# Square sums on GpSimd, a row norm for the memory, a reordered opening, two moved steps, and the turned probabilities of the differential heads on ScalarE

## The chip, the cores and the metric

One core of a Trainium2 chip runs the whole program once. The metric is the device time of one execution in microseconds (us), the median of three runs. The engines are PE (TensorE, matrix products), DVE (VectorE), ACT (ScalarE), POOL (GpSimd) and SP (SyncE, which here only issues DMAs). They run beside each other, each in the order of its own program, and meet at semaphores.

## What is computed

A transformer stack of width 1024 over 256 tokens, in float32, of which only the parts that the change touches are shown.

```python
def rmsnorm(x, g):
    xf = x.astype(jnp.float32)
    y = xf * lax.rsqrt(jnp.mean(xf * xf, axis=-1, keepdims=True) + EPS)
    return (y * g.astype(jnp.float32)).astype(x.dtype)

# first block
h = rmsnorm(x, norm_mix_g[l])
x = x + gated_branch_mixer(h, w_in[l], ...)              # begins with h @ w_in: a_val, a_gate, ...
x = x + memory_cross_attention(rmsnorm(x, norm_x_g[l]), rmsnorm(mem, norm_mem_g[l]), ...)
x = x + hierarchical_moe(rmsnorm(x, norm_ffn_g[l]), ...)  # 16 experts in 4 groups
# second block, layer 0 (sparse attention heads) and layer 1 (differential heads)
h = rms_norm(x, ln_mix_g[i]) * (1.0 + sc1[:, None, :]) + sh1[:, None, :]
x = x + g1[:, None, :] * y                                # y: the attention of the layer
h = rms_norm(x, ln_mlp_g[i]) * (1.0 + sc2[:, None, :]) + sh2[:, None, :]
x = x + g2[:, None, :] * (jnp.square(jax.nn.relu(h @ w_mlp_in[i])) @ w_mlp_out[i])
# differential heads: 8 heads of two softmaxes
p = masked_softmax(s, kpos[None, :] <= t[:, None])
a = p[:, :, 0] - lam * p[:, :, 1]
o = jnp.einsum('bhqk,bhkd->bhqd', a.astype(v.dtype), v)
o = rms_norm(o, subln_g) * (1.0 - lam_init)
```

`sc` and `sh` come from a product of a 1024-vector with a 1024x6144 matrix per layer (`w_ada`), the "modulation".

## The kernel before

**Products in three parts.** Activations lie turned: 128 features on the partitions, 256 tokens along the row, eight such blocks (KB = 8). A float32 product is made of three products of the fp32r type: high weights by high activations, high by low, low by high. ACT makes the high part of a weight panel (`w_hi`, `ahead`, line 1505) and of an activation, DVE the low part as the rest (`w_lo`, `ahead`, line 2045; `e_lo`, `h_lo`). A weight panel of 128x2048 elements (1 MB) is brought by a DMA on SP's queue (`load_panel`, line 515) into one of a ring of raw buffers, in the order of a plan. A panel's load waits until PE has finished with the panel that held the buffer. PE, ACT and DVE each go through the panels in the same order, and where in its program an engine makes its part of a panel is written out by hand.

**Norms.** For a norm over the 1024 features, ACT squares the blocks in pairs (128x512 each), and PE adds over the partitions by products with a matrix of ones, which leaves the sum on all partitions: `stat_pair(tag, j)` (line 847) waits for the j-th pair of squares and makes two products of 256 columns, so that a norm has 8. They stand between the panels that PE works on while the squares come in. ACT then takes the square root (`root`, line 1586) and DVE the reciprocal. Five norms, called x, ffn, m0, d and m1, are made "raw" (`raw_first`, line 729): PE doesn't wait for the square root but multiplies the residual, with its gains, and the factor is put on the result afterwards. For them ACT makes the high part of each block (`raw_act`, line 1546) and DVE the low one (`raw_low`, line 2109). PE takes each block with six products. The last pair of squares is waited for between the fourth block and the fifth; for d, later pairs stand behind the second, fourth and fifth block. `split_norm` (line 2084) is a norm that is not raw, `scaled` (line 2075) one whose result is not split.

**The opening.** SP's queue (`loads`, line 498) issues the identity, the two halves of x, panel 0, nine rows of small vectors, panel 1; then it waits until all 18 small vectors have landed (the other nine are on ACT's queue), issues the memory (1 MB), and goes on with panel 2. ACT gets the sums of squares of the rows of x by an accumulating square (128x1024, one per half). DVE puts their reciprocal roots on a diagonal, PE spreads them with the ones matrix and turns the small vectors, DVE takes them out of PSUM, splits panel 0 and makes the eight scaled blocks (`split_norm`, the call at line 2173). PE makes a_gate (two panels), then turns the memory in sixteen 128x128 transposes, and makes a_val. The memory's blocks are squared (`squares_of`), summed by 8 ones products behind a_val (`stats`, line 858), and scaled by `scaled("mem", ...)`; they are used after the gates, near 150 us.

**GpSimd** has little to do: it makes the windowed sums of the pooling branch (line 585), issues the 64 DMAs of the modulation matrix (`ada_loads`, line 608; each waits for DVE to have used the piece before), issues small constants, computes one gain vector (line 633), and makes the low part of two panels of d_o.

**The experts** (16, three panels each) run two deep. DVE and ACT make each expert's hidden activation, DVE multiplies it with the row of its gate, and PE needs its high (`e_hi`) and low part (`e_lo`). Pieces of the modulation (`ada(l, n)`, line 2450: 1 or 2 DVE operations of 128x1536 each) are put between DVE's other steps by hand, in the expert stage for layer 0, in the first MLP for layer 1.

**The differential heads.** Per head h: scores on PE, maxima on DVE (`d_max`), exponentials on ACT (`d_exp`, two), the normalized difference on DVE (`d_norm`, line 2840), three transposes on PE (`d_turned`) into PSUM, one copy of 128x384 out of it (on ACT for even h, on DVE for odd h), and the products with the values on PE (`d_values`, line 1419). Every second head ACT squares and copies the output of a pair of heads (`d_out`, line 1995). Behind the last head come a root, a reciprocal and spreads on PE, and the panels of d_o, with `keep_busy` products as filler where PE would stand still.

## Time and profile before

| what | value |
|---|---|
| time, median of 3 runs (lowest, highest) | 1316.54 us (1315.47, 1316.83) |
| the profiled execution: time | 1315.27 us |
| its span in the trace | 1313.5 us |
| PE busy | 1290.3 us, 98% |
| DVE busy | 950.7 us, 72% |
| ACT busy | 657.9 us, 50% |
| GpSimd busy | 88.5 us, 7% |
| chain that ended last, by engine | PE 86%, DVE 8%, ACT 3%, issue 2% |

The span is what the trace covers; the time of the same execution is 1.8 us longer. The granted TensorE clock was 0.998 of full speed. How a row of a timeline is read: start in us from the span's beginning, duration in us, engine, line of the kernel, operation, tile out<-tiles in, size out<-size in, and x with the number of instructions that the row covers; a bracket gives the engine's wait right before and what it waited for. In a group's row the numbers behind the bar are busy us, mean ns of one instruction, and idle us before them. `arena` is one large SBUF buffer that many stages share, so its name stands for different things in different rows; `ring` and `acc` are PSUM banks, and L675, L1503 are helpers that record most products and activations.

### The profile page before, as it was taken

To read this page: it belongs to the slowest core of one execution; us is meant where nothing else is said; L and a number is where in the kernel's file an instruction comes from. 1 tells how busy PE (TensorE), PEld (TensorE's weight loads), DVE (VectorE), ACT (ScalarE), POOL (GpSimd) and SP (SyncE) were. 2 spreads that over 40 slices of the span, in tenths; PEclk is the share of its full clock that TensorE was granted. 3 is DMA by queue.
4 is the path that set the end of the run, shared out by engine and by line. 5 is a ranking of instruction groups with operands and counts; after the bars stand their busy time and mean duration, and the time that the engine had idled before them with its cause. 6 is when DMAs were issued, how large, how long until landed. Compare 5 with 4: busy or idle time off the path is not lost.

```text
span 1313.5 us, 24511 instructions
## 1 busy us (share of the span) xinstructions
PE 1290.3 (98%) x10581; PEld 1237.9 (94%) x10581; DVE 950.7 (72%) x1199; ACT 657.9 (50%) x872; POOL 88.5 (7%) x134
## 2 busy tenths in 40 slices
PE   7999999999999999999999999999999999999998
PEld 7999999999999999999989689999999888999998
DVE  5769897764797667777776978877789666754443
ACT  4544436364643434343657747454456455654441
POOL 4003000000000000020100000100000020000000
PEclk9999999999999999999999999999999999999999
DMA  9665555545488777885632046999875431465550
GB/s 280 202 206 176 182 176 166 187 135 179 161 288 297 258 258 267 284 284 166 209 128 92 6 161 225 322 313 325 312 235 168 165 97 65 161 192 193 180 174 33
DMA packets 172701, 259.67 MB, mean 198 GB/s; under 512 B 5157, under 2 KB 147794, under 8 KB 172594
## 3 DMA queue, kind: packets, MB, share of 16 engines
q1 hardware_dynamic: 160906, 203.13, 47.1%
q0 software_dynamic: 10848, 53.69, 11.6%
q8 instruction: 84, 1.38, 0.4%
q10 hardware_dynamic: 840, 1.28, 0.3%
q14 instruction: 23, 0.19, 0.1%
HBM read 257.03 MB, written 1.05 MB: 196 GB/s over the span
## 4 chain that ended last, share of the span: by engine, by line
PE 86%; DVE 8%; ACT 3%; issue 2%; DMA 1%; SPq 0%; POOL 0%; ACTq 0%; DVEq 0%
PE ring L675 59%; PE acc L675 24%; ACT w_hi L1503 2%; DVE w_lo L2051 2%; PE acc L1276 1%; DVE arena L2100 1%; PE ring L1085 1%; DMA raw<-in_w_in_dram 1%; ACT h_hi L1503 1%; ACT arena L1503 1%; DMA arena<-in_w_ada_dram 1%; DVE arena L2464 0%; DVE h_lo L2096 0%; DVE h_lo L2094 0%; DVE norm L2066 0%
## 5 line engine op out<-in xcount | busy, mean ns | idle before, releaser
L675 PE MATMUL ring<-h_hi,w_hi 128*128 128x256 f32 (+1 forms) x2016 | 575.0, 285 | 5.7 <-DVE w_lo L2051 1.8
L675 PE MATMUL ring<-h_hi,w_lo 128*128 128x256 f32 (+1 forms) x2016 | 568.2, 282 | 0.0
L675 PE MATMUL ring<-h_lo,w_hi 128*128 128x256 f32 (+1 forms) x2016 | 566.5, 281 | 0.0
L2051 DVE TENSOR_TENSOR w_lo<-raw,w_hi 128x2048 fp32r<-128x2048 f32 x189 | 430.9, 2286 | 165.4 <-ACT w_hi L1503 164.7
L1503 ACT ACTIVATE w_hi<-raw 128x2048 fp32r<-128x2048 f32 x191 | 363.2, 1905 | 132.1 <-PE ring L675 64.0
L675 PEld LDWEIGHTS ring<-h_hi,w_hi 128*128 128x128 f32 x2016 | 379.8, 188 | 11.8 <-issue 7.3
L675 PEld LDWEIGHTS ring<-h_lo,w_hi 128*128 128x128 f32 x2016 | 380.7, 189 | 2.6 <-issue 2.2
L675 PEld LDWEIGHTS ring<-h_hi,w_lo 128*128 128x128 f32 x2016 | 380.9, 189 | 0.0
L675 PE MATMUL acc<-e_hi,w_hi 128*128 128x256 f32 x768 | 216.9, 282 | 2.9 <-DVE e_lo L2752 1.5
L675 PE MATMUL acc<-e_hi,w_lo 128*128 128x256 f32 x768 | 215.1, 280 | 0.0
L675 PE MATMUL acc<-e_lo,w_hi 128*128 128x256 f32 x768 | 215.1, 280 | 0.0
L1503 ACT ACTIVATE arena<-ring 128x512 f32<-128x512 f32 (+3 forms) x106 | 61.1, 582 | 245.0 <-PE ring L675 232.6
L675 PEld LDWEIGHTS acc<-e_hi,w_hi 128*128 128x128 f32 x768 | 144.4, 188 | 4.5 <-DVE e_lo L2499 1.8
L675 PEld LDWEIGHTS acc<-e_lo,w_hi 128*128 128x128 f32 x768 | 144.6, 188 | 0.0
L675 PEld LDWEIGHTS acc<-e_hi,w_lo 128*128 128x128 f32 x768 | 144.5, 188 | 0.0
L2464 DVE SCALAR_TENSOR_TENSOR arena<-arena,cond 128x1536 f32<-128x1536 f32 x56 | 101.6, 1813 | 5.8 <-DMA arena<-in_w_ada_dram 4.3
L606 POOL DMA_DIRECT2D arena<-in_w_ada_dram x64 | 33.8, 529 | 561.9 <-DVE arena L2464 327.4
L2752 DVE TENSOR_TENSOR e_lo<-arena,e_hi 128x512 fp32r<-128x512 f32 x32 | 22.1, 691 | 62.3 <-ACT e_hi L1503 62.3
L1503 ACT ACTIVATE e_hi<-arena 128x512 fp32r<-128x512 f32 x48 | 29.8, 621 | 63.4 <-DVE arena L2494 63.1
L2230 DVE SCALAR_TENSOR_TENSOR arena<-arena,vec 128x256 f32<-128x256 f32 x120 | 54.7, 524 | 0.0
L675 PE MATMUL ring<-arena 64*128 64x128 f32 (+5 forms) x370 | 52.0, 352 | 0.9 <-ACT arena L1503 0.8
L1503 ACT ACTIVATE arena<-ring,stat 128x128 f32<-128x128 f32 (+1 forms) x104 | 42.8, 428 | 16.8 <-DVE stat L2659 9.3
(317 smaller groups left out, 1348.2 us busy)
## 6 DMA issues: line engine op xcount, KB each, us to landing
arena<-in_w_ada_dram POOLq DMA_DIRECT2D x64, 768.0 KB, 6.3
raw<-in_w_mlp_in_dram SPq DMA_DIRECT2D x32, 1024.0 KB, 5.8
raw<-in_w_mlp_out_dram SPq DMA_DIRECT2D x32, 1024.0 KB, 5.0
raw<-in_w_in_dram SPq DMA_DIRECT2D x24, 1024.0 KB, 5.8
raw<-in_w_e_gate_dram SPq DMA_DIRECT2D x16, 1024.0 KB, 6.3
raw<-in_w_e_up_dram SPq DMA_DIRECT2D x16, 1024.0 KB, 5.4
raw<-in_w_e_down_dram SPq DMA_DIRECT2D x16, 1024.0 KB, 5.0
raw<-in_diff_w_in_dram SPq DMA_DIRECT2D x12, 1024.0 KB, 5.3
```

The costliest lines, as they stand in the source:

```text
L606: pool.dma_start(flat(ADA_RAW, (n % 2) * ADA_W, ADA_W), src).then_inc(S(f"ada_landed{n % 2}"), 16)
L675: return nc.tensor.matmul(dst, lhs, rhs, start=start, stop=stop, **kw)
L1085: last = nc.tensor.transpose(bank(f)[:, j * P:(j + 1) * P], src, ident[:])
L1276: last = nc.tensor.transpose(dst[:, c * P:(c + 1) * P], src[:, c * P:(c + 1) * P], ident[:])
L1503: return nc.scalar.activation(dst, src, fn, **kw)
L2051: tt(w_lo[q % RAW][:, 0:n], raw[q % RAW][:, 0:n], w_hi[q % SPL][:, 0:n].bitcast(F32), ALU.subtract)\
L2100: stt(blk(mid, 8)[:, b], x_t[:, b, :], gain(b), norm[:, row, :], ALU.mult, ALU.mult)\
L2230: chain.did(stt(y[:, b], at, w, y[:, b], ALU.mult, ALU.add))
L2464: last = stt(done_at if k == KB - 1 else so_far, piece, cond[:, k:k + 1], so_far, ALU.mult, ALU.add)
L2752: tt(e_lo[:, s, :].rearrange("p b t -> p (b t)"), hid(2 + c % 2), e_hi[:, s, :].rearrange("p b t -> p (b t)").bitcast(F32), ALU.subtract). ...
```

## The change

**Square sums.** For the norms x, ffn, m0, d and m1, GpSimd adds the squares of the first six blocks: `fold_two` adds pair 1 to pair 0 (128x512), `fold_rest` adds pair 2 (128x512) and then the two halves of the result (128x256). PE then makes one product with the ones matrix for that sum and two for the last pair: `stat_sums`, at the place in `raw_first` where the last pair was before (for d: behind the seventh block). All `stat_pair` calls go, and the function too.

**Where GpSimd does it.** x: ahead of the wait for `xo_ready`. ffn: inside `ada_loads(0)`, behind the second piece's DMA. m0: inside `ada_loads(1)`, `fold_two` behind the fourth piece, `fold_rest` behind the pieces ahead of the loop. d: behind `ada_loads(1)`. m1: behind the two splits of d_o.

**The mix norm's gain** gets a transpose of its own (`mix_gain`, 8 columns), so that the norm doesn't wait for all small vectors. DVE makes the norm's first two blocks, then the low part of panel 0, then the rest; the take-out of the other vectors comes behind panel 1. Panel 1 is split in two halves (ACT and DVE), and PE starts on the first as soon as it is there (`two_halves`).

**The memory** is normed by rows: ACT makes accumulating squares of the landed rows (two of 128x1024) and a root, DVE a reciprocal and two row scalings of 128x1024, PE turns the scaled rows, and DVE multiplies each block with its gain as it takes it out of PSUM (8 of 128x256 in place of 4 of 128x512). The 8 ones products, `squares_of("mem")`, `root("mem")` and `scaled("mem")` go. SP's queue issues panel 2 ahead of the memory's DMA.

**Two orders.** In the expert stage the split of the panel behind the first expert's moves ahead of the wait for the gate row, on DVE and on ACT, and one modulation piece moves behind the product with the gate row. In the MLP `chunk_lo(1)` moves ahead of the modulation piece `ada(1, 4)`.

**The differential heads.** ACT makes the PSUM copy of every head, DVE none. Some semaphores become several in turn (`sig`), with no other effect.

```diff
 def loads
             load_panel(sp, turn, 1)
-            sp.wait_ge(S("vecs_landed"), 16 * N_VEC_DMA)
+            sp.wait_ge(S("vecs_landed"), 16 * (N_VEC_DMA - 1))
+            load_panel(sp, turn, 2)
 on GpSimd
+            def fold_two(tag):
+                pool.wait_ge(*sig(tag + "_squared", 2))
+                nc.gpsimd.tensor_tensor(sq[:, 0:2], sq[:, 0:2], sq[:, 2:4], ALU.add).then_inc(S(tag + "_folded"), 1)
+            def fold_rest(tag):
+                pool.wait_ge(*sig(tag + "_squared", 3))
+                pool.wait_ge(*sig(tag + "_folded", 1))
+                nc.gpsimd.tensor_tensor(sq[:, 0:2], sq[:, 0:2], sq[:, 4:6], ALU.add).then_inc(S(tag + "_folded"), 1)
+                pool.wait_ge(*sig(tag + "_folded", 2))
+                nc.gpsimd.tensor_tensor(sq[:, 0], sq[:, 0], sq[:, 1], ALU.add).then_inc(S(tag + "_folded"), 1)
 ada_loads
                     ada_load(turn, l, n, at(n))
+                    if n == (1, 3)[l]:
+                        fold_two(("ffn", "m0")[l])
+                        if l == 0:
+                            fold_rest("ffn")
+                if l == 1:
+                    fold_rest("m0")
 raw_first on PE
-                    for j in sums.get(k, ()):
-                        stat_pair(tag, j)
+                    if k == sums:
+                        stat_sums(tag)
+            def stat_sums(tag):
+                f, sq = FL[tag + "_stat"], blk(SQX, 8)
+                open_fill(f)
+                pe.wait_ge(*sig(tag + "_folded", 3))
+                mm(bank(f)[:, 0:T], ones[:], sq[:, 0], True, False)
+                pe.wait_ge(*sig(tag + "_squared", 4))
+                mm(bank(f)[:, 0:T], ones[:], sq[:, 6], False, False)
+                mm(bank(f)[:, 0:T], ones[:], sq[:, 7], False, True).then_inc(S(tag + "_summed"), 1)
 PE, the opening
-            keep_busy(FL["a_gate"], 8)
-            full("a_gate", split="mix_ready", together=1)
-            pe.wait_ge(S("mem_landed"), 16)
+            keep_busy(FL["a_gate"], 4)
+            linear_first([PN["a_gate"]], FL["a_gate"], block_ready("mix_ready"))
+            two_halves(PN["a_gate"] + 1, FL["a_gate"] + 1)
+            pe.wait_ge(S("mem_rows"), 2)
             turn_rows(lambda i: acc[i], 2048, "mem_turned")
             full("a_val")
-            stats("mem", lambda k: blk(SQ + k)[:, 0], "mem_squared")
 PE, three of the places of the sums
-            raw_first("ffn", PN["moe"], half_bank(moe_fill(0)), {3: (3,)})
+            raw_first("ffn", PN["moe"], half_bank(moe_fill(0)), 3)
-                raw_first(f"m{l}", PN[name], lambda b: acc[b], {3: (3,)})
+                raw_first(f"m{l}", PN[name], lambda b: acc[b], 3)
-            raw_first("d", PN["d_q"], lambda b: acc[b], {1: (0, 1), 3: (2,), 4: (3,)})
+            raw_first("d", PN["d_q"], lambda b: acc[b], 6)
 ACT, the opening
-            ahead(2 - SPL)
+            act.wait_ge(S("raw_landed1"), 16)
+            for b, sem in ((0, "first_half_hi"), (1, "hi_made")):
+                c = slice(b * P, (b + 1) * P)
+                func(w_hi[1][:].rearrange("p (k n) -> p k n", k=KB)[:, :, c], raw[1][:].rearrange("p (k n) -> p k n", k=KB)[:, :, c],
+                     ACT.Copy).then_inc(S(sem), 1)
+            act.wait_ge(S("mix_ready"), KB)
+            act.wait_ge(S("mem_landed"), 16)
+            for t in range(2):
+                last = func(blk(SQ + 4 * t, 4), arena[:, 2048 + t * D:2048 + (t + 1) * D].rearrange("p (b t) -> p b t", b=4),
+                            ACT.Square, accum_out=stat[:, 4 + t:5 + t])
+            func(stat[:, 6:8], stat[:, 4:6], ACT.Sqrt, scale=1.0 / D, bias=eps[:]).then_inc(S("mem_squared"), 1)
             ahead(0)
 DVE, the opening
+            split_norm("mix", lambda b: mix_gain[:, b:b + 1], mid=SQ, row=2, behind_two=lambda: ahead(1 - SPL))
+            dve.wait_ge(S("mem_squared"), 2)
+            chain.did(nc.vector.reciprocal(stat[:, 6:8], stat[:, 6:8]))
+            chain.settle()
+            for t in range(2):
+                rows = arena[:, 2048 + t * D:2048 + (t + 1) * D]
+                ts(rows, rows, stat[:, 6 + t:7 + t], None, ALU.mult).then_inc(S("mem_rows"), 1)
 DVE, the experts
+            ahead(PN["moe"] + 1)
             dve.wait_ge(S("cond_made"), 1)
-            for n in range(2):
-                ada(0, n)
+            ada(0, 0)
             row_wait(0)
             tt(act0, act0, row, ALU.mult).then_inc(S("act_made"), 1)
-            ahead(PN["moe"] + 1)
+            ada(0, 1)
             expert_lo(0)
 DVE, the MLP
                 ahead(PN[name] + 1)
+                chunk_lo(1)
                 if l == 0:
                     ada(1, 4)
-                chunk_lo(1)
                 ahead(PN[name] + 2)
 ACT, the differential heads
             for h in range(DIFF_HEADS):
-                if h % 2 == 0:
-                    act.wait_ge(S("d_turned"), h + 1)
-                    func(d_pt(h), acc[2][:, 0:3 * P], ACT.Copy).then_inc(S("d_pt_even"), 1)
-                elif h > 2:
+                act.wait_ge(S("d_turned"), h + 1)
+                func(d_pt(h), acc[2 + h % 2][:, 0:3 * P], ACT.Copy).then_inc(S(("d_pt_even", "d_pt_odd")[h % 2]), 1)
+                if h % 2 and h > 2:
                     d_out(h // 2 - 1)
 DVE, the differential heads
-                if h % 2:
-                    dve.wait_ge(S("d_turned"), h + 1)
-                    nc.vector.tensor_copy(d_pt(h), acc[3][:, 0:3 * P]).then_inc(S("d_pt_odd"), 1)
```

## Rows read from the trace of the kernel before

**Rows 1.** The page: busy time by engine, and one of its costliest groups.
```profile
PE 1290.3 (98%) x10581; PEld 1237.9 (94%) x10581; DVE 950.7 (72%) x1199; ACT 657.9 (50%) x872; POOL 88.5 (7%) x134
...
L2051 DVE TENSOR_TENSOR w_lo<-raw,w_hi 128x2048 fp32r<-128x2048 f32 x189 | 430.9, 2286 | 165.4 <-ACT w_hi L1503 164.7
```

**Rows 2.** PE's timeline: start us, duration us, instruction; in brackets the wait before.
```profile
26.29 0.39 PE L675 MATMUL ring<-h_hi,w_hi 128*128 128x256 f32 x1 [1.84 <-DVE w_lo L2051]
...
338.54 0.35 PE L675 MATMUL ring<-h_hi,w_hi 128*128 128x256 f32 x1 [1.03 <-DVE h_lo L2094]
...
362.94 0.39 PE L675 MATMUL acc<-e_hi,w_hi 128*128 128x256 f32 x1 [1.18 <-DVE e_lo L2499]
...
819.26 0.39 PE L675 MATMUL acc<-e_hi,w_hi 128*128 128x256 f32 x1 [1.52 <-DVE e_lo L2752]
```

**Rows 3.** PE's timeline: products with the ones matrix.
```profile
45.25 3.62 PE L675 MATMUL ring<-arena,k_ones 128*128 128x256 f32 x16
...
268.41 1.03 PE L675 MATMUL ring<-arena,k_ones 128*128 128x256 f32 x4
...
796.67 1.13 PE L675 MATMUL ring<-arena,k_ones 128*128 128x256 f32 x4
...
1127.11 1.13 PE L675 MATMUL ring<-arena,k_ones 128*128 128x256 f32 x4
```

**Rows 4.** GpSimd's groups by line and shape: busy us, mean ns, idle before.
```profile
L633 POOL TENSOR_TENSOR f_gain<-vec 128x8 f32<-128x8 f32 x1 | 2.3, 2284 | 0.0
...
L585 POOL TENSOR_TENSOR arena<-u_pad 128x1084 f32<-128x1084 f32 x1 | 2.0, 1987 | 78.8 <-issue 78.8
...
L585 POOL TENSOR_TENSOR arena<-arena 128x257 f32<-128x257 f32 x1 | 0.8, 801 | 0.1
```

**Rows 5.** DVE's timeline in the convolution.
```profile
99.34 8.25 DVE L2230 SCALAR_TENSOR_TENSOR arena<-arena,vec 128x256 f32<-128x256 f32 x8
...
115.02 3.25 DVE L2230 SCALAR_TENSOR_TENSOR arena<-arena,vec 128x256 f32<-128x256 f32 x8
```

**Rows 6.** ACT's timeline near the x and ffn sums.
```profile
267.06 0.62 ACT L1503 ACTIVATE arena<-x_t 128x512 f32<-128x512 f32 x1
...
334.70 0.47 ACT L1503 ACTIVATE norm<-ring,eps 128x256 f32<-128x256 f32 x1 [0.84 <-PE ring L675]
```

**Rows 7.** DVE's and ACT's timelines before the m0 sum.
```profile
791.90 2.46 DVE L2116 SCALAR_TENSOR_TENSOR h_lo<-x_t,mod_g,h_hi 128x256 fp32r<-128x256 f32 x6
...
796.00 0.62 ACT L1503 ACTIVATE arena<-x_t 128x512 f32<-128x512 f32 x1
```

**Rows 8.** DVE's and ACT's timelines in the d norm.
```profile
986.99 4.48 DVE L2051 TENSOR_TENSOR w_lo<-raw,w_hi 128x2048 fp32r<-128x2048 f32 x2
...
1002.07 0.71 ACT L1503 ACTIVATE arena<-arena,k_scaled 128x512 f32<-128x512 f32 x1
```

**Rows 9.** The memory's DMA issue; DVE's and ACT's timelines in the opening.
```profile
arena<-in_mem_dram SPq DMA_DIRECT2D x1, 1024.0 KB, 8.8
...
16.54 0.88 DVE L2100 SCALAR_TENSOR_TENSOR arena<-x_t,vec,norm 128x256 f32<-128x256 f32 x2
...
6.37 1.04 ACT L1503 ACTIVATE arena<-arena 128x1024 f32<-128x1024 f32 x1
...
26.96 1.92 ACT L1503 ACTIVATE w_hi<-raw 128x2048 fp32r<-128x2048 f32 x1 [3.05 <-DMA raw<-in_w_in_dram]
```

**Rows 10.** DVE's timeline in the expert stage and the MLP.
```profile
354.84 1.01 DVE L2462 TENSOR_SCALAR arena<-arena,cond 128x1536 f32<-128x1536 f32 x1
...
359.39 0.69 DVE L2523 TENSOR_TENSOR arena<-arena 128x512 f32<-128x512 f32 x1 [1.61 <-ACT arena L1503]
...
818.52 0.68 DVE L2752 TENSOR_TENSOR e_lo<-arena,e_hi 128x512 fp32r<-128x512 f32 x1
```

**Rows 11.** PE's and ACT's timelines in the differential heads.
```profile
1088.02 0.52 PE L1276 MATMUL acc<-k_ident,arena 128*128 128x128 f32 x3 [0.30 <-DVE arena L2853]
...
1087.32 1.09 ACT L1503 ACTIVATE arena<-acc 128x512 f32<-128x512 f32 x2 [0.32 <-PE acc L675]
```

More of the change, by code:

```diff
@@ L242, in fill_plan @@
     first, count, at = {}, {}, 0
-    for name, n in (("x_t", 4), ("a_gate", 2), ("a_val", 2), ("mem_stat", 1),
+    for name, n in (("x_t", 4), ("mix_gain", 1), ("a_gate", 2), ("a_val", 2),
                     ("c_x", 2), ("c_c", 2), ("c_b", 2), ("u_pool", 2), ("gates", 12), ("x_k", 4), ("x_v", 1), ("ln_stat", 1), ("x_v1", 1), ("lv_stat", 1),
@@ L2073, in sums_wait, with split_norm @@
                     dve.wait_ge(S("panel_done"), p + 1)
-            def scaled(tag, src, dst, gain, nb=KB):
-                inverse(tag)
-                chain.settle()
-                for b in range(nb):
-                    last = stt(dst(b), src(b), gain(b), norm[:, 2, :], ALU.mult, ALU.mult)
-                    if b % 2:
-                        last.then_inc(S(tag + "_scaled"), 1)
-            def split_norm(tag, gain, shift=None, mid=SQX, row=None):
+            def split_norm(tag, gain, shift=None, mid=SQX, row=None, behind_two=None):
                 if row is None:
@@ L2102, in split_norm @@
                     if b == 1:
+                        if behind_two is not None:
+                            behind_two()
                         low(0)
```

122 lines of the change are left out of this document (70 added, 52 removed).

## The prediction

> **What bounds the kernel now.** I read the page first: PE is busy for 1290.3 of 1313.5 us [rows 1], so time can only come from work that leaves PE or from the 23 us in which it waits. The second view is PE's timeline, filtered for waits. The four rows that this change touches are a wait of 1.84 us for the second weight panel of the opening, 1.03 us for the first normalized block of the expert stage, 1.18 and 1.52 us for the low halves of activations (e_lo) [rows 2]. The third view is ACT's and DVE's timelines around each norm: a matmul that leaves PE is a gain only where PE, and not the ACT and DVE chain beside it, ends last.
>
> **Square sums.** A product with the ones matrix is two records; the 16 records of the memory's sum end 3.62 us after the first starts, the last one lasting 0.38, so they stand 0.216 us apart and one product costs 0.432 us [rows 3]. Each of the five norms x, ffn, m0, d, m1 goes from 8 products to 3 (2.16 us), and the memory's 8 go altogether (3.46 us): 33 products, 14.3 us of PE's work.
>
> What is added is three GpSimd additions per norm: twice 128x512, once 128x256. The trace has none of 512. The one of 1084 took 1.99 us with DVE idle, 1.84 ns an element, which gives 0.94 and 0.47 us; the one of 257 took 0.80 us beside DVE's work [rows 4]. So a fold costs GpSimd 2.35 us, or up to 3.1 us if the small ones keep their price beside DVE. GpSimd's own queue has room: the ffn fold stands ahead of DMAs that wait for DVE anyway, and the m0 fold holds back pieces used 20 us later.
>
> The rows also show that it isn't beside DVE for free. The conv's 128x256 operations take 8.25 us for eight while GpSimd adds, and 3.25 us for eight when it doesn't [rows 5]; and a GpSimd product of 8 elements took 2.28 us [rows 4], as long as the weight split DVE was then running [rows 1]. I read this as one engine standing still until the other's instruction is over. The Trainium skill, SBUF — State Buffer (section "SBUF: two separate sides"), says just this: a GpSimd instruction that reads SBUF and a DVE one with two SBUF inputs take an exclusive lock. By that rule the trace agrees; an account that only counts PE would miss it.
>
> Norm by norm, with t for the old time:
> - x. PE reached its last pair of products at 268.41 [rows 3], though ACT had the last squares at 267.68 (267.06 + 0.62) [rows 6]. With the earlier products gone PE comes 1.7 us sooner but must still wait for these squares, since ACT and DVE are in step with each other and not with PE. Gain 0.7 at most, not 2.16. The second and third additions (1.4 us) fall on the six low blocks, with 0.5 us of slack behind them and 0.4 in front: 0.5 us later. Net -0.2.
> - ffn. DVE and ACT follow PE here. The square root ran at 334.70 [rows 6] when PE's sum came, the first expert block at 338.54 after it [rows 2]; both move with PE by 2.2 us, and the additions fall into DVE's gaps. Net -2.2.
> - m0. PE's last pair began at 796.67 [rows 3], just when ACT's last squares were done (796.00 + 0.62) [rows 7]. This chain is DVE's: six lows from 791.90 in one go [rows 7], the last residual, ACT's highs and squares. All of PE's 2.16 us become a wait. The additions land on these lows: 0.2 + 0.94 + 0.47 = 1.6 us later.
> - m1. The same picture (PE's last pair at 1127.11 [rows 3], as the squares were done); DVE is idle when the second addition starts, so 1.0 us less 0.3 of slack: +0.7.
> - d. PE-bound at first, so 2.16 us are free there. But DVE runs lows, two weight splits (986.99, 4.48 us for both) and the reciprocal without a gap [rows 8]. Nearly all additions fall on the lows, so everything behind is 1.9 us later: the first rotated block, ready from ACT at 1002.07 + 0.71 = 1002.78 [rows 8], comes at 1004.7, where PE wanted it at 1004.26 before. Net +0.5 (without contention -1.5).
>
> **Row norm of the memory and the opening.** The norm now waits for one small DMA and not for 18: DVE's first scaling, at 16.54 [rows 9], can start near 13.0, but the split of panel 0 (2.29 us) is put behind two of its steps, so PE starts 1.6 us sooner. The half-wise split of panel 1 takes out the 1.84 us wait [rows 2]. So a_gate ends some 3.5 us sooner, near 28.5. Then PE needs the memory's scaled rows. On SP's queue the memory's DMA is moved behind panel 2. Before, it landed 8.8 us after 13.99, at 22.8, and panel 2 at 26.96 [rows 9]; the queue carries the same bytes, so the memory now lands near 26.9. Behind it: two squares (1.04 each plus accumulator reads, 2.2), root and reciprocal (0.5), two scalings of 1024 elements at 1.01 us per 1536 [rows 10], so 1.4: ready at 31.1; sixteen transposes to 33.0. ACT's split of panel 2 (1.9) stands behind the root and DVE's behind the scalings: 29.5 + 1.9 + 2.3 = 33.7. The first a_val product was at 33.77. Gain 0.1 us; 2.7 us more if the memory lands at 24, 3 us less if it lands behind panel 3. The 3.46 us of the memory's sum are then a full gain, as PE has no wait for 100 us after it and DVE loses 8 scalings and a reciprocal there. The tail of the gates waits as before.
>
> **Two orders.** In the expert stage DVE's split of a panel moves into the time when it waited for the gate rows; its product with the rows stays at 359.39 [rows 10]. Between it and e_lo stood a split (2.29), now one modulation piece (1.82): -0.5 of the 1.18 us. In the MLP e_lo moves ahead of a modulation piece. It ran at 818.52 [rows 10]; without the piece it can run 1.7 us sooner, and ACT's half is there by then: all 1.52 us go, -1.5.
>
> **Differential heads.** DVE loses four copies (0.47 each). ACT gets them, each 0.4 us and, worse, a wait for the head's transposes in front of the squares of earlier heads. A list of the three engines' steps with durations from the rows gives the transposes of heads 3 to 6 up to 0.2 us sooner, head 7 (1088.02 [rows 11]) 0.4 later, because the exponentials stand behind copy and squares. Then the tail: the squares of heads 4 and 5 ran at 1087.32 [rows 11], before that transpose; now behind it and its copy, ending near 1090, so the table load and root behind them and the first spread come 1.1 us later, and PE has only filler. Net +1.1 (-0.4 if I have ACT too slow, +1.7 at worst).
>
> **The sum.** -0.1 - 3.5 - 0.2 - 2.2 - 0.5 + (1.6 - 1.5) + 0.5 + 0.7 + 1.1 = -4.1 us. The profiled run took 1315.27 us, the span plus 1.8, which is 1.3 below the median of 1316.54. Against that median: 1312.4 us. Its own range, from the bounds of the terms, is 1309.5 to 1315.
>
> **Rivals.**
> - The fold runs free of DVE (rows 5 could be the conv's own pattern). Then x -0.7, m0 -1.5, d -1.5, m1 0: -8.9 us, 1307.6. Chance 0.18.
> - The memory lands early: forecast less 2.7, 1309.7. For it: larger packets than a panel's. Chance 0.12.
> - PE counts alone: 14.3 + 3.5 + 2.0 = 19.8, 1296.7. Against it stand rows 6 and 7. Chance 0.05.
> - The memory lands behind panel 3: +3, 1315.4, no change to speak of. Chance 0.07.
> - Slower: the lock at full price. Each addition holds DVE for what it takes beside work (3.1 us a fold), and the last one of d misses its place and waits behind a weight split (2.3), so PE's sum and all behind it do. x +2.4, m0 +1.6, d +3.9, m1 +2.7, heads +1.7, against ffn -1.7, expert -0.5, memory -3.6: +6.5, 1323.0. It decides once a fold costs DVE's chains over some 2.6 us. Row 2.28 of [rows 4] speaks for it, the gaps in x and m1 against. Chance 0.08.
> The forecast has 0.50. That GpSimd's sums never enter (the change not doing what it says) I exclude: PE waits on them.
>
> **Chances and range.** 0.2% (2.6 us) is about what a measurement can tell from no change. Of the forecast's 0.50, 0.35 lies below 1313.9. Faster 0.35 + 0.18 + 0.12 + 0.05 = 0.70; same 0.15 + 0.07 = 0.22; slower 0.08. The range that leaves out under 2 in 10 reaches from below the free fold to past the median: 1305.5 to 1316.5.
>
> **What would show it.** Records of 256-wide products with the ones matrix fall from 128 to 62. GpSimd additions of 512 at 0.9 to 1.2 us, and DVE's lows of m0, d and m1 near 0.8 us where they overlap them. A new PE wait of over 1 us in x, m0 and m1 ahead of the last squares. A PE wait of 2 to 3 us for the memory's rows near 29. The wait of 1.52 us gone. A PE wait or filler 1 us longer ahead of d_o. If lows keep 0.41 us, the lock is wrong; if the memory's squares start at 24, the queue is; if a_val starts after 35, the opening is worse than I say.

## The result, and the profile after

The changed kernel took 1319.26 us (median of 9 runs, 1316.48 to 1321.94) against 1316.32 us (9 runs, 1315.37 to 1317.27): a ratio of 1.0025 with a 95% interval from 1.0016 to 1.0033. It is slower by 0.25%, where 0.3% faster was forecast, and it lies outside the range of 1305.5 to 1316.5 us.

The profiled execution took 1319.08 us, its span 1317.3 us. The page's busy times, after:

```profile
PE 1283.1 (97%) x10510; PEld 1230.9 (93%) x10510; DVE 953.2 (72%) x1195; ACT 655.9 (50%) x874; POOL 107.6 (8%) x149
```

PE is busy 7.2 us less than in [rows 1] and the span is 3.8 us longer, so PE stands 11 us more. PE's timeline, filtered for waits, shows where (start, duration, instruction, in brackets the wait before it):

```profile
262.31 1.13 PE L703 MATMUL ring<-arena,k_ones 128*128 128x256 f32 x4 [0.80 <-ACT arena L1541]
...
330.46 0.35 PE L703 MATMUL ring<-h_hi,w_hi 128*128 128x256 f32 x1 [1.03 <-DVE h_lo L2134]
...
354.38 0.38 PE L703 MATMUL acc<-e_hi,w_hi 128*128 128x256 f32 x1 [0.71 <-DVE e_lo L2555]
...
367.16 0.36 PE L703 MATMUL ring<-h_hi,w_hi 128*128 128x256 f32 x1 [1.19 <-DVE arena L2544]
...
789.70 0.36 PE L703 MATMUL acc<-h_hi,w_hi 128*128 128x258 f32 x1 [2.86 <-DVE h_lo L2158]
...
830.72 0.87 PE L1127 MATMUL ring<-k_ident,arena 128*128 128x128 f32 x6 [3.63 <-DVE arena L2520]
...
1005.86 1.10 PE L703 MATMUL ring<-arena,k_rotate 128*128 128x512 f32 x2 [1.25 <-ACT arena L1541]
...
1090.18 0.52 PE L1318 MATMUL acc<-k_ident,arena 128*128 128x128 f32 x3 [1.20 <-DVE arena L2909]
...
1126.11 0.36 PE L703 MATMUL acc<-h_hi,w_hi 128*128 128x258 f32 x1 [1.94 <-DVE h_lo L2158]
...
1130.72 1.13 PE L703 MATMUL ring<-arena,k_ones 128*128 128x256 f32 x4 [0.98 <-ACT arena L1541]
```

The waits of 1.84 and 1.52 us of [rows 2] are gone, that of 1.18 is 0.71. New are those ahead of the last squares of x and m1 (0.80 and 0.98), three for low blocks or rotated ones (2.86 us in m0, 1.25 in d, 1.94 in m1), one of 3.63 us in the MLP, and one of 1.19 in the experts; the wait ahead of head 7 has grown from 0.30 to 1.20. The wait of 3.63 us is for the transposes that turn a finished row of the modulation, which had no wait in the kernel before.

**Stage by stage.** SP issues a panel's load when PE has finished the panel that held its buffer. The start of the same load in both timelines of SP's queue is therefore a clock hand of PE. After minus before, in the two profiled executions:

| stage that ends here (us, before) | after - before | the stage's part | forecast |
|---|---|---|---|
| a_val (39.7) | -2.63 | -2.6 | -0.1 |
| the memory's sum (54.6) | -6.08 | -3.5 | -3.5 |
| the x norm (272.3) | -5.99 | +0.1 | -0.2 |
| the ffn norm (337.5) | -8.07 | -2.1 | -2.2 |
| first expert's hidden part (368.9) | -8.56 | -0.5 | -0.5 |
| the expert behind it (380.3) | -7.15 | +1.4 | 0 |
| all experts, first projections (641.6) | -7.43 | -0.3 | 0 |
| sparse heads (718.3) | -4.30 | +3.1 | 0 |
| the m0 norm (800.7) | -2.10 | +2.2 | +1.6 |
| second chunk of the MLP (825.3) | -3.83 | -1.7 | -1.5 |
| the turned modulation (837.3) | +1.53 | +5.4 | 0 |
| rest of the MLP (942.9) | +1.28 | -0.3 | 0 |
| the d norm (1011.0) | +1.67 | +0.4 | +0.5 |
| differential heads (1108.7) | +2.65 | +1.0 | +1.1 |
| the m1 norm (1131.2) | +3.64 | +1.0 | +0.7 |
| the end | +3.8 | +0.2 | 0 |

Twelve of the sixteen rows came out within 0.6 us of the forecast. Three that it had at 0 carry +9.9 us: the expert behind the first, the sparse heads and the turned modulation. The opening is off by 2.5 us the other way.

**The clock.** The view of stretches (us from to, length, PE busy with its records, granted clock, DMA share, GB/s) shows where after had less than full speed; the last fence is the kernel before.

```profile
699.00:702.00 3.00, 3.00 (x16) 0.50 0.00 0
702.00:705.00 3.00, 3.00 (x17) 0.50 0.00 0
705.00:708.00 3.00, 3.00 (x19) 0.50 0.00 0
...
786.00:789.00 3.00, 0.84 (x8) 1.00 0.45 133
789.00:792.00 3.00, 2.30 (x14) 0.80 1.04 322
792.00:795.00 3.00, 3.00 (x16) 0.63 0.93 369
...
828.00:831.00 3.00, 0.28 (x3) 1.00 0.88 329
831.00:834.00 3.00, 3.00 (x20) 0.62 1.08 341
834.00:837.00 3.00, 3.00 (x23) 0.81 0.48 188
```

```profile
708.00:711.00 3.00, 3.00 (x20) 0.58 0.03 5
```

The granted clock was 0.50, the lower of the two levels (1.2 of 2.4 GHz), for some 10 us near 700, and for some 3.4 us each behind the waits of 2.86 and 3.63 us. In us of full speed that is 5.1, 1.7 and 1.7. The kernel before lost 1.7 near 708 and nothing in the other two places. So the 3.1 us of the row "sparse heads" are this difference in the clock, and not a wait: PE's timeline has no gap there in either kernel. And 1.7 us of "the turned modulation" are the clock behind the wait.

How far one profile is from the mean is seen from the runs, of which each has its time and mean granted clock. A least-squares fit over all runs of this study (one constant for each kernel, one slope for all) gives 0.95 us for each 0.001 of clock, with 1.0 us of scatter left in a run. The kernel before had a mean clock of 0.9966 (55 runs with a clock on record, 0.995 to 0.999; the profiled one 0.998), the changed one 0.9933 (9 runs, 0.991 to 0.997). That difference is 3.1 us. At the same clock the changed kernel is 0.2 us faster, with 0.4 us of uncertainty (one standard error), so that the two can't be told apart. The result has thus two halves: what the change won was eaten by new waits, and the clock behind two of these waits made it slower. Two columns below use this fit: "mean clock", and "at the same clock", which is the constant of the kernel less that of the kernel before.

### The profile page after: what moved, and what is told of

Same layout as the page of the kernel before. It is cut to its first block, busy times and chain, and to the rows that moved or that the text cites. A ratio compares the mean times of both kernels' runs of the same rounds, so it can differ in the third digit from the quotient of the medians.

```text
span 1317.3 us, 24386 instructions
## 1 busy us (share of the span) xinstructions
PE 1283.1 (97%) x10510; PEld 1230.9 (93%) x10510; DVE 953.2 (72%) x1195; ACT 655.9 (50%) x874; POOL 107.6 (8%) x149
## 3 DMA queue, kind: packets, MB, share of 16 engines
q10 hardware_dynamic: 840, 1.28, 0.3%
## 4 chain that ended last, share of the span: by engine, by line
PE 80%; DVE 10%; ACT 3%; DMA 3%; issue 3%; SPq 0%; POOL 0%; POOLq 0%; DVEq 0%; ACTq 0%
PE ring L703 55%; PE acc L703 23%; DVE w_lo L2100 3%; DMA arena<-in_w_ada_dram 2%; ACT w_hi L1541 1%; PE acc L1318 1%; ACT arena L1541 1%; DVE h_lo L2158 1%; DMA arena<-in_mem_dram 1%; DVE arena L2140 1%; PE ring L1127 1%; DVE arena L2520 1%; DVE h_lo L2136 1%; ACT h_hi L1541 1%; DMA vec_in<-in_nsa_pe_v_dram 0%
## 5 line engine op out<-in xcount | busy, mean ns | idle before, releaser
L2100 DVE TENSOR_TENSOR w_lo<-raw,w_hi 128x2048 fp32r<-128x2048 f32 (+1 forms) x188 | 428.9, 2288 | 162.6 <-ACT w_hi L1541 162.2
```

The source lines that it names most:

```text
L2100: tt(w_lo[q % RAW][:, 0:n], raw[q % RAW][:, 0:n], w_hi[q % SPL][:, 0:n].bitcast(F32), ALU.subtract)\
```

## The experiments

| kernel | time, us | ratio to before (95%) | mean clock | at the same clock |
|---|---|---|---|---|
| changed | 1319.26 | 1.0025 (1.0016 to 1.0033) | 0.9933 | -0.2 |
| mlp_order_back | 1314.69 | 0.9983 (0.9973 to 0.9994) | 0.9956 | -3.0 |
| piece_ahead | 1317.51 | 1.0008 (0.9998 to 1.0019) | 0.9935 | -1.8 |
| m0_on_pe | 1318.14 | 1.0009 (1.0001 to 1.0018) | 0.9944 | -0.5 |
| opening_alone | 1312.67 | 0.9963 (0.9950 to 0.9976) | 0.9966 | -4.2 |
| three_mended | 1312.21 | 0.9957 (0.9944 to 0.9970) | 0.9964 | -5.4 |
| kept_parts | 1310.13 | 0.9952 (0.9939 to 0.9964) | 0.9952 | -7.8 |
| heads_back | 1318.37 | 1.0014 (1.0003 to 1.0024) | 0.9941 | -0.3 |
| kept_memory_first | 1307.61 | 0.9934 (0.9921 to 0.9947) | 0.9978 | -8.0 |
| additions_beside | 1309.33 | 0.9947 (0.9933 to 0.9960) | 0.9980 | -5.8 |
| piece_in_gap | 1307.24 | 0.9929 (0.9916 to 0.9943) | 0.9968 | -9.1 |

Times are medians of 5 to 12 runs. The last column is uncertain by some 0.3 us at 12 runs and 0.5 at 5; these are single standard errors, and a difference between two rows needs about 1.3 us (both of 5 runs) to be clear. The ratios are to the runs of the kernel before that were taken with each kernel.

### The MLP's order put back

```diff
                 ahead(PN[name] + 1)
-                chunk_lo(1)
                 if l == 0:
                     ada(1, 4)
+                chunk_lo(1)
```

> The changed kernel with one order put back: in the MLP the modulation piece stands ahead of the second chunk's low part again. Theory A (the piece used later makes the transfers of its successors start in the middle of a weight panel's): PE's wait of 3.63 us for the turned modulation goes, and with it the stretch at a lower granted clock behind it (1.7 us); the wait of 1.5 us for the low half comes back. 3.6 + 1.7 - 1.5 = 3.8 us less than the changed kernel: 1315.4 us. Theory B (the pieces are late because GpSimd issues them behind the additions of m0): the wait of over 2 us stays and 1.5 us are added: 1319 to 1321 us.

4.6 us less than the changed kernel, where 3.8 were expected. In its PE timeline the wait of 1.52 us is back and there is none of over 0.3 us near 830; the clock is full there.

```profile
818.92 0.39 PE L703 MATMUL acc<-e_hi,w_hi 128*128 128x256 f32 x1 [1.52 <-DVE e_lo L2808]
```

Theory A holds. What happened is seen on three queues. The piece 7 of the modulation, the one that completes the row, can be loaded only when piece 5 was used. In after, GpSimd issued it at 821.68, 0.25 us behind a panel's load on SP's queue, and DVE stood 3.06 us until 828.84:

```profile
821.68 0.53 POOL L622 DMA_DIRECT2D arena<-in_w_ada_dram  x1 [3.40 <-DVE arena L2520]
...
821.43 0.37 SPq L523 DMA_DIRECT2D raw<-in_w_mlp_out_dram  x1
...
828.84 1.82 DVE L2520 SCALAR_TENSOR_TENSOR arena<-arena,cond 128x1536 f32<-128x1536 f32 x1 [3.06 <-DMA arena<-in_w_ada_dram]
```

In the kernel before the same piece was issued at 823.78, between the panels' loads of 817.77 and 825.26, and DVE took it up at 828.38 after 0.71 us:

```profile
823.78 0.53 POOL L606 DMA_DIRECT2D arena<-in_w_ada_dram  x1 [4.00 <-DVE arena L2464]
...
828.38 1.82 DVE L2464 SCALAR_TENSOR_TENSOR arena<-arena,cond 128x1536 f32<-128x1536 f32 x1 [0.71 <-DMA arena<-in_w_ada_dram]
```

4.6 us in the one case and 7.2 in the other, from issue to use: the order let PE and SP run 1.7 us ahead, the pieces didn't follow, and the transfer met a panel's. PE, 3.8 us earlier than before at this place, stood until the row was there; in the kernel before the last piece ended at 830.20 and the transposes began at 830.76, without a wait. The other profiles bear this out: in the four kernels with the new order (changed, piece_ahead, m0_on_pe, heads_back) this transfer was issued 0.25 to 0.32 us behind a panel's and landed 6.8 to 8.1 us later; in seven with the old one the last panel's lay 6.0 us back, and it landed after 4.5 to 5.5. That the edit causes the wait is shown by this experiment; that the meeting of the two transfers makes the landing late is read from the timelines, since no run moved the transfer alone.

### Both pieces ahead of the gate row in the expert stage

```diff
             ahead(PN["moe"] + 1)
             dve.wait_ge(S("cond_made"), 1)
-            ada(0, 0)
+            for n in range(2):
+                ada(0, n)
             row_wait(0)
...
             tt(act0, act0, row, ALU.mult).then_inc(S("act_made"), 1)
-            ada(0, 1)
             expert_lo(0)
```

> The changed kernel with both modulation pieces of the expert stage ahead of the product with the gate row again, while the split of the next panel stays where the change put it. Theory A (the second piece used later, at 353.7 us, starts the transfer of the piece after next 4 us later, DVE stands 1.92 us for it and PE 1.19): both waits go, and the wait for the first low half stays under 0.8 us: 1.2 us less than the changed kernel, 1318.0 us. Theory B (the split ahead is what shifts the transfers): both waits stay, 1319.3 us.

1.8 us less in the median, 1.6 at the same clock, where 1.2 were expected. In the shift by panels its stage behind the first expert is at -8.31 us and stays there, while after goes from -8.56 to -7.15. Theory A again: in after DVE was done with the second piece at 353.72, the next load was issued at 354.02, 0.3 us behind a panel's, and DVE could take it up only at 362.39, after a wait. In the run here PE's wait of 1.19 us is gone, and that of 0.71 us for the low half is 0.29. The profiled execution shows no gain at the end all the same: it is 1.1 us ahead of after at 718 us and has lost that at m0, where PE waits 4.08 us and not 2.86. DVE has two pieces of the modulation to do ahead of m0's low blocks, waits for their transfers, and isn't there sooner than in after. That the runs are faster by more than the 1.2 us rests on the medians and the fit.

```profile
354.02 0.53 POOL L622 DMA_DIRECT2D arena<-in_w_ada_dram  x1 [3.18 <-DVE arena L2520]
...
353.71 0.37 SPq L523 DMA_DIRECT2D raw<-in_w_e_up_dram  x1
...
362.39 1.82 DVE L2520 SCALAR_TENSOR_TENSOR arena<-arena,cond 128x1536 f32<-128x1536 f32 x1 [1.92 <-DMA arena<-in_w_ada_dram]
```

### The m0 sum on PE again

The eight products and their places as in the kernel before, no addition on GpSimd for m0; the other folds stay.

> The changed kernel with the squares of the m0 norm summed by eight products on PE again and no addition on GpSimd there. Theory A (PE's stand of 2.86 us for the low blocks comes from the products that are gone and from DVE shared with GpSimd, and the lower granted clock after it, 1.7 us, comes from that stand): PE's wait is under 0.5 us, the clock stays full near 790 us, DVE's six low blocks take 2.5 and not 2.9 us: 2.2 us less than the changed kernel, 1317.0 us. Theory B (the clock fell there by chance): 0.6 us less, 1318.6 us, and a stretch at a lower clock near 790 us as before.

1.1 us less in the median, between the two. The trace takes theory A's side: DVE's six low blocks are back at 2.46 us, PE waits only 0.30 us there, ahead of the last squares, the clock is full, and the stage costs 0.3 us in place of 2.2. But the wait for the turned modulation is there as before, behind a stage that GpSimd no longer holds up:

```profile
829.21 1.29 PE L1138 MATMUL ring<-k_ident,arena 128*128 128x128 f32 x6 [3.34 <-DVE arena L2532]
```

That excludes theory B of the first experiment as well. Why only 1.1 us of some 1.9 show in the time isn't settled. At the same clock it is only 0.3 us, with 0.4 us of uncertainty: nearly all of the gain shows as clock (0.9944 against 0.9933).

### The opening alone

Sums, orders and heads as in the kernel before.

> Only the opening and the row norm of the memory as changed; sums, orders and heads as in the kernel before. Theory A (these two parts are worth what the time of the panels shows up to 60 us, 6.1 us, and nothing takes it back): 1310.2 us, the clock in the sparse heads as in the kernel before. Theory B (the longer stretch at the lower clock near 700 us comes with an earlier arrival there, whatever the cause): 3.1 us of it are taken back, 1313.3 us, with a granted clock near 0.5 for some 9 us near 700 us.

3.5 us less than the kernel before in the median, between the theories. At the same clock it is worth 4.2 us, where the forecast had 3.6 and the profile of after 6.1. The profiled executions say why it scatters. ACT squares the memory as soon as it has landed, in after at 24.40 us, here at 26.29:

```profile
24.40 1.06 ACT L1541 ACTIVATE arena<-arena 128x1024 f32<-128x1024 f32 x1 [1.92 <-DMA arena<-in_mem_dram]
```

```profile
26.29 1.06 ACT L1549 ACTIVATE arena<-arena 128x1024 f32<-128x1024 f32 x1 [4.74 <-DMA arena<-in_mem_dram]
...
30.52 3.48 PE L918 MATMUL acc<-k_ident,arena 128*128 128x128 f32 x16 [2.57 <-DVE arena L2238]
```

```profile
30.00:32.00 2.00, 1.48 (x7) 0.57 1.11 349
```

Here PE waits 2.57 us for the scaled rows, the clock falls behind it (the last fence, a stretch of 2 us in the view of stretches), and the opening gains 0.0 us up to a_val in place of 2.6. Eight profiled kernels have this opening: the memory was squared between 24.4 and 26.5 us, and PE waited 1.6 to 2.6 us for the rows in six of them, not at all in two, of which the changed kernel's own is one. Up to a_val these eight gained between 2.6 us and nothing (one lost 0.3), with 0.5 us in the middle. The long stretch near 700 us is in this profile too (5.1 us of full speed), so the profile alone would speak for theory B. But the mean clock over the five runs is 0.9966, that of the kernel before: an earlier arrival doesn't lower the clock there as a rule.

### Three faults mended, and only the gains kept

`three_mended` is the changed kernel with the three edits above together. `kept_parts` has, beyond that, the sums of x, d and m1 on PE and the copies of the odd heads on DVE: of the change it keeps the opening with the row norm, the fold of ffn, and the split ahead in the expert stage.

> The changed kernel with the MLP order back, both modulation pieces of the expert stage ahead of the gate row again, and m0 summed on PE; the folds of x, ffn, d and m1, the opening and the heads stay as changed. Theory A (the three faults lie in different stages and their costs add, the lower granted clock with them): 4.6 us (measured alone) + 1.7 (measured alone) + 1.2 (measured alone) = 7.5 us less than the changed kernel, 1311.8 us, mean clock as in the kernel before (0.9966). Theory B (the lower clock belongs to the changed kernel as a whole and returns at other places): 1315 us with a mean clock of 0.994.

> Only the parts that the traces show to gain: the opening with the row norm, the fold of ffn, the panel split ahead in the expert stage (both pieces ahead of the gate row); m0, x, d, m1, the MLP order and the heads as in the kernel before. From the run of the opening alone, 1312.7 us, less 2.1 us for ffn and 0.4 for the split: Theory A 1310.2 us. Theory B (PE that comes earlier to a stage finds a later part not ready, so that what is won in front is lost behind): 1312 us or more, with a new PE wait behind 340 us.

Both theories A hold: 1312.21 us (1311.8 expected) at a mean clock of 0.9964, and 1310.13 us (1310.2 expected). The difference at the same clock, 2.4 us, is the price of the folds of x, d and m1 and of the heads, for which the table of stages has 0.1 + 0.4 + 1.0 + 1.0 = 2.5; with five runs each it is uncertain by 0.6.

### The copies of the odd heads back on DVE

> The changed kernel with the copies of the odd differential heads on DVE again. Theory A (the copies behind squares on ACT make the transposes of head 7, the root and the spreads 1 us later): 1.0 us less than the changed kernel, 1318.3 us, the wait ahead of head 7's transposes 0.3 and not 1.2 us. Theory B (the later time there is inherited from the stages before): no change, 1319.3 us, both waits stay.

0.9 us less in the median, 0.1 at the same clock, so the time can't tell. The trace can: from the d norm to d_o the shift against the kernel before goes from +3.77 to +3.75 us, in after from +1.67 to +2.65, and the wait ahead of head 7 is 0.30 us again. In after ACT took the last copy and both squares in one go, and the table load behind them came at 1092.22:

```profile
1090.74 1.47 ACT L1541 ACTIVATE arena<-acc 128x384 f32<-128x384 f32 x3 [2.10 <-PE acc L1318]
1092.22 1.28 ACT L1541 ACT_TABLE_LOAD   x1
```

In the kernel before the squares ran at 1087.32 [rows 11] and the table load right behind them:

```profile
1088.42 1.28 ACT L1503 ACT_TABLE_LOAD   x1
```

### The memory ahead of panel 2

```diff
             sp.wait_ge(S("vecs_landed"), 16 * (N_VEC_DMA - 1))
-            load_panel(sp, turn, 2)
             m_rows = a["mem"][0].rearrange("(t p) n -> p t n", p=P)
             sp.dma_start(...).then_inc(S("mem_landed"), 16)
+            load_panel(sp, turn, 2)
```

> The kept parts, with the memory's DMA ahead of panel 2 on SP's queue as in the kernel before. Theory A (PE's wait of 0 to 2.6 us for the memory's rows near 29 us is the landing of the memory behind panel 2, and the stretch at the lower clock at 30 us follows this wait): the memory lands near 22.8 and not 24.4 to 26.3 us, the wait and that stretch go, 1 to 2 us less than the kept parts: 1308.7 us. Theory B (panel 2, which then lands near 27 us, is needed by the first product behind the transposes): PE waits as long for its low half, no gain, 1310.2 us.

2.5 us less than the kept parts, with 1.1 us of uncertainty (five runs each). ACT squares the memory at 23.33 us, PE has no wait of over 0.2 us from 17 to 40 us, and there is no stretch at the lower clock near 30. In the shift by panels the profile has -6.25 us behind the memory's sum, where that of kept_parts has -4.02, so 2.2 us are won in the opening. At the same clock it is 0.2 us better, so that nearly all of the gain shows as clock: 0.9978 against 0.9952. Of this difference of 0.0026 the lost stretch in the opening (1.7 us) explains half; the two profiles differ by as much again near 700 us (3.4 and 1.7 us lost), which the order has no part in, so a part of the 2.5 us may be luck. Theory B has its part: in the two kernels below, which have this order too, PE waited 0.88 and 1.64 us for the low half of panel 2, with the clock full behind it. They squared the memory at 21.65 and 24.25 us, so the order doesn't fix the landing either.

```profile
23.33 1.06 ACT L1551 ACTIVATE arena<-arena 128x1024 f32<-128x1024 f32 x1 [0.73 <-DMA arena<-in_mem_dram]
```

### The additions alone

```diff
+            def extra_two(tag):
+                pool.wait_ge(*sig(tag + "_squared", 2))
+                nc.gpsimd.tensor_tensor(extra, sq[:, 0:2], sq[:, 2:4], ALU.add).then_inc(S(tag + "_folded"), 1)
...
+                if j == 3 and tag in ("m0", "d", "m1"):
+                    pe.wait_ge(*sig(tag + "_folded", 3))
```

The base is `kept_memory_first`; `extra` is a part of a buffer that is free then, and PE's sums read the squares as before.

> The kept parts with the memory first (1307.6 us), and at m0, d and m1 the three GpSimd additions of the changed kernel once more, written to a place that nobody reads; PE keeps all eight products of these norms and waits for the additions before the last pair. What is measured is the price of the additions alone. Theory A (an addition and DVE's operations hold each other up): DVE's small low part and six low blocks of m0 take some 4.2 us (1.24 + 2.93) and not 2.6, everything behind is later: m0 +1.5, d +0.4 to 1.9, m1 +1.0, together 3 to 4 us: 1311 us. Theory B (what the changed kernel lost there came from PE, which waits where its products had been, and from the clock): 0 to 0.5 us, 1307.9 us, the six low blocks at 2.46 us.

1.7 us more than its base, 2.1 at the same clock (0.6 of uncertainty); between the theories in time. In the shift by panels against the base m0 costs 2.0, d 0.2 and m1 0.8 us, 3.0 together, as theory A has it. DVE's small low part and six low blocks take 1.16 and 2.84 us, 4.0 together where theory A has 4.2. That d costs so little fits the prediction, which had 1.5 us between the rotated block (1002.78) and PE's need of it (1004.26). The timelines of DVE and GpSimd show how m0 comes about:

```profile
782.62 1.80 DVE L2554 SCALAR_TENSOR_TENSOR arena<-arena,cond 128x1536 f32<-128x1536 f32 x1
784.34 1.16 DVE L2190 TENSOR_TENSOR h_lo<-mod,h_hi 128x16 fp32r<-128x16 f32 x1
785.43 2.84 DVE L2192 SCALAR_TENSOR_TENSOR h_lo<-x_t,mod_g,h_hi 128x256 fp32r<-128x256 f32 x6
...
783.44 2.03 POOL L625 TENSOR_TENSOR c_pad<-c_pad,arena 128x512 f32<-128x512 f32 x1 [3.69 <-ACT arena L1574]
...
790.57 1.13 PE L715 MATMUL ring<-arena,k_ones 128*128 128x256 f32 x4 [1.38 <-ACT arena L1574]
```

The addition starts while DVE works on the modulation piece, takes 2.03 us, and ends at 785.47. DVE's piece is not longer for it (1.80 us), but its next operation, 16 elements that take 0.17 us otherwise, takes 1.16 and ends at 785.50, with the addition. So the addition stood for most of the time that the piece still ran, and the small operation while the addition ran. That is the exclusive lock which the Trainium skill states (SBUF — State Buffer, section "SBUF: two separate sides"): of a GpSimd instruction that reads SBUF and a DVE one with two SBUF inputs, the one that starts first holds the other up until it is over. The trace agrees with it but for 0.25 us: an addition of 1.30 us that stood until the piece's end at 784.42 would have ended at 785.72.

### The piece in the gap

```diff
             def mlp(l, before):
                 name = f"mlp{l}"
+                if l == 0:
+                    ada(1, 4)
                 inverse(f"m{l}")
...
                 ahead(PN[name] + 1)
-                if l == 0:
-                    ada(1, 4)
                 chunk_lo(1)
```

> The kept parts with the memory first (1307.6 us); the modulation piece that stood ahead of the second chunk's low part in the MLP moves ahead of m0's reciprocal, where DVE waits 1.91 us for ACT's root. Theory A (only the piece's place made PE wait 1.52 us near 818 us, and a piece used early starts the transfers of its successors early, so that none is late): the wait of 1.52 us goes and none of over 1 us comes near 830 us: 1306.1 us. Theory B (PE's order there is such that the turned modulation is next in line whatever the pieces do): a wait of 1 us or more near 820 to 830 us takes its place, 1307.6 us or more. Theory C (the piece is longer than the gap or lands late there): the reciprocal and all behind it come later by what it exceeds, at 1.73 us in 1.91 us nothing.

0.4 us less than its base in the median, 1.1 at the same clock (its mean clock was 0.001 lower, with 5.1 us lost near 700 in its profile, and 1.64 for panel 2 in the opening). The piece fits, the reciprocal waits 0.18 us for ACT's root, and the wait of 1.52 us is gone; 0.49 us of wait for the turned modulation are left, where theory B wanted over 1.

```profile
791.35 1.81 DVE L2531 SCALAR_TENSOR_TENSOR arena<-arena,cond 128x1536 f32<-128x1536 f32 x1
793.34 1.75 DVE L2126 RECIPROCAL norm<-norm 128x256 f32<-128x256 f32 x1 [0.18 <-ACT norm L1551]
...
824.52 0.87 PE L1133 MATMUL ring<-k_ident,arena 128*128 128x128 f32 x6 [0.49 <-DVE arena L2531]
```

With 1307.24 us, 0.7% under the kernel before, it is the best of the kernels here, though the last step alone isn't clear of the scatter.

## Why the prediction was wrong

**What held.** PE's count of 33 products was not the gain, as [rows 6, 7] said: x lost 0.1 us where PE had 2.16 us less to do, with a new wait of 0.80 us for the last squares. The memory's sum gave its full 3.5 us, ffn 2.1, and d, m1 and the heads cost 0.4, 1.0 and 1.0 us, all within 0.3 of their terms. m0 cost 2.2 where 1.6 was said; the additions by themselves cost 2.0 there (`additions_beside`). A fold took 3.4 us with DVE idle in part and up to 5.2 beside it, where 2.35 to 3.1 was said. GpSimd's groups by shape, after:

```profile
L607 POOL TENSOR_TENSOR arena<-arena 128x512 f32<-128x512 f32 x5 | 7.7, 1531 | 234.6 <-ACT arena L1541 234.6
L612 POOL TENSOR_TENSOR arena<-arena 128x512 f32<-128x512 f32 x5 | 7.2, 1445 | 16.6 <-ACT arena L1541 16.5 <-POOL arena L607 0.2
L614 POOL TENSOR_TENSOR arena<-arena 128x256 f32<-128x256 f32 x5 | 4.3, 856 | 0.4
```

That size was too low by over a quarter: the nanoseconds per element of the longest addition in [rows 4] don't carry over to 512 elements (1.30 us with DVE idle, 0.94 said). The kernel before had an addition much nearer in size, which would have given 1.10:

```profile
L585 POOL TENSOR_TENSOR arena<-arena 128x530 f32<-128x530 f32 x1 | 1.1, 1137 | 0.1
```

It cost little, since what counts is which DVE operation lies beside it.

**What failed: the step "Two orders".** It priced the wait that goes, and got that right: -0.5 and -1.5 us said, -0.5 and -1.7 measured. It gave no price to what a moved piece issues. A piece of the modulation isn't only 1.8 us of DVE. Its use frees the buffer for the piece after next, so that its place sets when that transfer starts, against PE's and SP's progress. In the expert stage the second piece went behind a product, in the MLP behind `chunk_lo(1)`, while the same edits brought PE and SP forward. Both times the next load fell right behind a panel's. The runs put the price at 1.6 us for the first (`piece_ahead`) and 2.8 us for the second, both at the same clock, the second net of the 1.5 us that the order wins (`mlp_order_back`); in the medians, with the clock, it is 1.8 and 4.6. Together with m0 they turn the sum: three_mended is 5.2 us better than the changed kernel at the same clock. The sentence that a piece behind the m0 fold is "used 20 us later" was right and beside the point: with no m0 fold the wait was still 3.34 us.

**What was missing: a term for the clock.** The prediction foresaw new PE waits in m0 and for the memory's rows, and priced each at its length. The profiles show what comes on top (the wait of 2.9 us ahead of the very first product, in every kernel, is left out; the clock was full behind it):

| PE's wait, us (kernel) | full speed lost behind it |
|---|---|
| 1.52 (before, in the MLP); 1.84 (before), 1.60 (mlp_order_back) and 1.64 (piece_in_gap), all in the opening | none |
| 1.94 or 1.95, in m1, in the changed kernel and five others | none |
| 1.87 (three_mended), 2.08 (kept_parts), 2.18 (m0_on_pe), 2.44 (heads_back), 2.57 (opening_alone), all in the opening | 1.7 us each |
| 2.86 (changed), 2.57 (heads_back), 3.36 (mlp_order_back), 4.08 (piece_ahead), in m0 | 1.7 us each |
| 3.63 (changed), 3.29 (piece_ahead), 3.34 (m0_on_pe), 4.56 (heads_back), turned modulation | 1.7 us each |

In these profiles nothing was lost behind the waits of up to 1.84 us, and something behind each from 2.08 us on; between them the length alone doesn't decide. That the waits are the cause is shown where an edit took one away: the stretch went with it in `mlp_order_back`, `m0_on_pe` and `kept_memory_first`. Where PE isn't the bound right behind, as in m0, this loss is hidden at least in part; behind the turned modulation, with 100 us of products that PE does without a wait, it is paid in full. By the means of the runs the clock makes up 3.1 of the 7.0 us between forecast and result.

**The opening** was forecast at -0.1 with a rival at -2.7 more. Both are seen: 0.0 in one profiled execution, -2.6 in another, -0.5 in the middle of eight, by when the memory is there (24.4 to 26.5 us, where 26.9 and 24 had been the two cases). The mechanism was right; it wasn't one value, and that the changed kernel's own profile has -2.6 is luck. Its wait cost clock besides. The order on SP's queue that the change made (panel 2 ahead of the memory) has at least a part in it: with the old order none of the three profiles has a wait for the rows, and the medians differ by 2.5 us.

**The rivals.** The one that ended slower was the lock at full price. That is not what happened: the folds cost about what the likeliest case said, and the slower result came by a way that no rival named. At 0.08 for slower, the chances rested on the folds alone and left the moved pieces without a case of their own.

**What stays open:** why the clock falls near 700 us, in the sparse heads, where PE's timeline shows no gap. Every profile has it, with 1.7 us of full speed lost in the kernel before and in kept_memory_first, 3.4 in five others and 5.1 in five, the changed one's among these. It probably makes much of the scatter from run to run, and no part of the change is its cause as far as the runs show: the kernel before has a mean clock of 0.9966, which is a loss of 4.5 us of full speed, while its profile shows 3.2. The changed kernel's clock is 0.0033 lower than that. The two new stretches (1.7 us each in 1317) account for 0.0026 of it, the one behind the memory's rows, where it occurs, for 0.0013.

## What to carry to other kernels

A step that is moved takes its transfers along: ask for each moved use of a buffer when the next load into it can start, and what is on the DMA queues then, above all when the same edit lets another engine run ahead. Work taken off the bounding engine in front of a chain that another engine sets becomes a wait, and a long wait can cost more than its length through the clock behind it, so such work is better left as filler. Put movable pieces where an engine already stands idle: the reciprocal's wait of 1.91 us took in a whole piece, and 0.18 us of it were left.

## What the runs showed of the hardware

- The mean granted clock of one and the same kernel went from 0.995 to 0.999 over 55 runs of the kernel before, and over all kernels the time followed with 0.95 us for each 0.001. The runs of that kernel differ by 4.7 us, in good part for this reason (1313.96 to 1318.68), so that a difference of 1 us needs either many runs or a comparison at the same clock.
- Lower clock came in portions: 1.7, 3.4 or 5.1 us of full speed lost in a place, in all twelve profiles (the last microseconds of a kernel apart).
- A GpSimd addition of 128x512 took 1.30 us with DVE idle and 2.03 to 2.13 us when it began under a DVE operation of 1.80 us. DVE's operation kept its time, and the next one, of 0.17 us, took 1.16 to 1.24. An addition that began first kept its 1.3 us, and DVE's operation of 0.47 us that began under it took 1.21 (the x norm of the changed kernel).
- A transfer of 768 KB landed 4.5 to 5.5 us after its issue when the last panel's load (1 MB, on SP's queue) had been issued 6.0 us before and the next followed 1.4 or 1.5 us later (seven kernels at the same place in the MLP), and 6.8 to 8.1 us after it when it was issued 0.25 to 0.32 us behind one (changed, piece_ahead, m0_on_pe, heads_back). In the expert stage of the changed kernel, 0.3 us behind one, it took 8.4 us from issue to use.
